# Attention scores of two softmax maps in three PSUM banks, and two banks in turn for transposed probabilities

## What the program must compute

```python
# group A: differential attention, per head; q and k split into two halves of 32
s1 = q[..., :32] @ k[..., :32].T * 32 ** -0.5
s2 = q[..., 32:] @ k[..., 32:].T * 32 ** -0.5
p  = softmax(s1) - lam * softmax(s2);      out_A = p @ v
# group D: attention over 512 latent keys with a window bias, and 256 context keys
p  = softmax(concat(q @ k_lat.T * 64 ** -0.5 + bias, q @ k_ctx.T * 64 ** -0.5));  out_D = p @ v
```

## Time and profile before

| | us |
|---|---|
| median of 3 executions | 5679.43 |
| lowest, highest | 5677.08, 5681.0 |
| the profiled execution | 5667.12 |
| its span, from first to last instruction | 5665.2 |
| `attend_stage` of layer 0, from the first product | about 450 to 676 |
| `attend_stage` of layer 1, from the first product | about 3633 to 3808 |

### The profile page before, as it was taken

The page is one execution under the profiler, slowest core; times in us unless marked ns, Lnnn a source line. Parts: engine busy times, 40 slices in busy tenths (PEclk is TensorE's granted clock), DMA queues, the critical chain, the costliest instruction groups (busy, mean ns, idle before and its releaser), DMA issues. The chain is left out here.

```text
span 5665.2 us, 93013 instructions
## 1 busy us (share of the span) xinstructions
PE 4687.9 (83%) x35878; PEld 2642.5 (47%) x35878; DVE 3514.7 (62%) x7609; ACT 1966.5 (35%) x5447; POOL 1761.5 (31%) x1767
## 2 busy tenths in 40 slices
PE   7988799768888797978877698779976978888777
PEld 3555599644334342524322255459964534334222
DVE  2776543468767677676764557554347776867644
ACT  1333333114343333434333223343321434343333
POOL 0210022004544444444443202003211454444432
PEclk8998899889999999999999999879988999999999
DMA  8756422429999999999999887312243999999998
GB/s 294 263 198 244 178 56 86 145 103 421 421 421 420 420 416 421 413 419 420 415 422 421 337 289 241 122 39 73 86 144 152 418 422 421 421 421 415 421 421 353
DMA packets 386541, 1729.76 MB, mean 305 GB/s; under 512 B 86216, under 2 KB 158456, under 8 KB 217976
## 3 DMA queue, kind: packets, MB, share of 16 engines
q0 software_dynamic: 195200, 1381.22, 59.3%
q1 hardware_dynamic: 163208, 281.69, 14.4%
q10 hardware_dynamic: 27696, 60.92, 3.0%
HBM read 1640.75 MB, written 86.65 MB: 305 GB/s over the span
## 5 line engine op out<-in xcount | busy, mean ns | idle before, releaser
L2419 PE MATMUL pe_ps<-pe_ring,pe_diag 128*128 128x512 f32 x5120 | 2455.0, 614 | 608.3 <-ACT pe_diag L2453 601.4
L2487 DVE SCALAR_TENSOR_TENSOR pe_ring<-pe_ring,ro_tb 128x1024 f32<-128x1024 f32 x1280 | 1561.5, 1225 | 935.0 <-DMA pe_ring<-in_peer_uv,ro_slot 913.5
L2066 POOL DMA_INDIRECT pe_ring<-in_peer_uv,ro_slot x1280 | 1443.3, 1128 | 2222.3 <-PE pe_ps L2419 1749.2
L2419 PEld LDWEIGHTS pe_ps<-pe_ring,pe_diag 128*128 128x128 f32 x5120 | 899.9, 191 | 2053.5 <-ACT pe_diag L2453 1326.9
L2447 ACT ACTIVATE pe_wts<-pe_raw 128x1 f32<-128x1 f32 x1280 | 258.4, 202 | 1744.9 <-DVE pe_ring L2487 1744.0
L929 PE MATMUL pp_ps<-pp_win,pp_uT 128*128 128x439 f32 (+6 forms) x1728 | 597.1, 504 | 8.0 <-issue 7.5
L2453 ACT ACTIVATE pe_diag<-c_ident,pe_wts 128x128 f32<-128x128 f32 x1280 | 513.9, 401 | 42.0
L929 PEld LDWEIGHTS pp_ps<-pp_win,pp_uT 128*128 128x128 f32 x1728 | 326.5, 195 | 263.9 <-issue 173.1
L2449 ACT ACTIVATE pe_wts<-pe_wts,ro_gates 128x1 f32<-128x1 f32 x1280 | 376.6, 294 | 41.6
L1372 POOL TENSOR_TENSOR ch_m<-ch_at,ch_joins 128x256 f32<-128x256 f32 x288 | 203.8, 744 | 472.6 <-DVE ch_at L1671 472.6
L2122 PEld LDWEIGHTS pe_ps<-ro_tbT,peer_wq 128*128 128x128 f32 x2048 | 248.8, 192 | 61.2 <-issue 61.2
(11 more groups left out here) (358 smaller groups left out, 5155.7 us busy)
## 6 DMA issues: line engine op xcount, KB each, us to landing
pp_win<-in_w_in SPq DMA_DIRECT2D x24, 1756.0 KB, 10.8
at_aw<-in_w_ada SPq DMA_DIRECT2D x10, 4096.0 KB, 13.3
pe_ring<-in_peer_uv,ro_slot POOLq DMA_INDIRECT x1280
ch_nat<-gd_dram SPq DMA_DIRECT2D x44, 448.0 KB, 4.1
gd_dram<-pp_gout POOLq DMA_DIRECT2D x40, 448.0 KB, 8.2
peer_wq<-in_peer_wq SPq DMA_DIRECT2D x8, 2048.0 KB, 8.5
rw_dram<-pp_out POOLq DMA_DIRECT2D x48, 320.0 KB, 5.2
ch_nat<-rw_dram SPq DMA_DIRECT2D x48, 320.0 KB, 4.1
```

The lines of the kernel that those rows point to most:

```text
L2066: return pool.indirect_dma_start(dst, None, table, bass.IndirectOffsetOnAxis(ap=index, axis=0))
L2419: mm = pe.matmul(ps[:, y_bank(p) + c, :], diag[:, n % DIAGS, :], ring[:, n % RING, D + c * 512:D + (c + 1) * 512], start=(k == 0), stop=(k ...
L2487: v.scalar_tensor_tensor(row, row, 1.0, tb[p % 2][:], ALU.mult, ALU.mult, accum_out=raw[p % 2][:, k:k + 1]).then_inc(dots_done, 1)
```

## The change

It has three edits. The two maps of group A are laid side by side in banks 0 to 2, 768 columns each, so that map 0 ends and map 1 begins in the middle of bank 1. `score_A` of a latent pair is issued in another order: map 0 keys 0 to 511 (bank 0), map 1 keys 256 to 767 (bank 2), map 0 keys 512 to 767 (the first half of bank 1); then PE waits for its own semaphore until that last product is done, and issues map 1 keys 0 to 255 (the second half of bank 1). Bank 3, which this leaves free, becomes a second bank for transposed probabilities: groups of transposes take banks 6 and 3 in turns, and each waits for the copy of the group before the last one only.

```diff
-        slotsA = ps[:, 0:4].rearrange("p (u a) b -> p u (a b)", u=2)
+        slotsA = ps[:, 0:3].rearrange("p a b -> p (a b)").rearrange("p (u k) -> p u k", u=2)
         slotD = ps[:, 4:6].rearrange("p a b -> p (a b)")
         ada_out = ps[:, 5, 256:512]
-        TURN, OUT = 6, 7
+        TURNS, OUT = (6, 3), 7
+        turn_bank = lambda job: TURNS[turn_at[job] % 2]
 ...
                 def score_A(x):
                     i, h = pairs[x]
                     if x:
                         pe.wait_ge(expA_done, 2 * x)
-                    for c0 in range(0, keys_of(x), 512):
-                        c1 = min(keys_of(x), c0 + 512)
-                        for u in range(2):
-                            at = 64 * (h % 2) + 32 * u
-                            mm = pe.matmul(slotsA[:, u, c0:c1], b["qA"][at:at + 32, h // 2, i * P:(i + 1) * P], b["kA"][at:at + 32, h // 2, c0:c1], start=True, stop=True)
-                            if c1 == keys_of(x):
-                                mm.then_inc(scoreA_done, 1)
+                    def map_scores(u, c0, c1):
+                        at = 64 * (h % 2) + 32 * u
+                        return pe.matmul(slotsA[:, u, c0:c1], b["qA"][at:at + 32, h // 2, i * P:(i + 1) * P], b["kA"][at:at + 32, h // 2, c0:c1], start=True, stop=True)
+                    if keys_of(x) == TOK:
+                        map_scores(0, 0, 512)
+                        map_scores(1, 256, TOK)
+                        map_scores(0, 512, TOK).then_inc(scoreA_done, 1)
+                        pe.wait_ge(scoreA_done, 2 * x + 1)
+                        map_scores(1, 0, 256).then_inc(scoreA_done, 1)
+                    else:
+                        map_scores(0, 0, CTX).then_inc(scoreA_done, 1)
+                        map_scores(1, 0, CTX).then_inc(scoreA_done, 1)
 ...
                 def turn(x, g, k):
                     n = turn_at[(x, g, k)]
                     pe.wait_ge((probsA_ready, probsD_ready)[g], x + 1)
-                    if n:
-                        pe.wait_ge(pt_ready, n)
+                    if n >= 2:
+                        pe.wait_ge(pt_ready, n - 1)
                     first, end = groups_of(x)[k]
                     for kt in range(first, end):
-                        tr = pe.transpose(ps[:, TURN, (kt - first) * P:(kt - first + 1) * P], ...
+                        tr = pe.transpose(ps[:, turn_bank((x, g, k)), (kt - first) * P:(kt - first + 1) * P], ...
```

More of the change, by code:

```diff
@@ L506, in turn @@
                     pe.wait_ge((probsA_ready, probsD_ready)[g], x + 1)
-                    if n:
-                        pe.wait_ge(pt_ready, n)
+                    if n >= 2:
+                        pe.wait_ge(pt_ready, n - 1)
                     first, end = groups_of(x)[k]
                     for kt in range(first, end):
-                        tr = pe.transpose(ps[:, TURN, (kt - first) * P:(kt - first + 1) * P], (pA, pD)[g][x % 2][:, kt * P:(kt + 1) * P], consts["ident"][:])
+                        tr = pe.transpose(ps[:, turn_bank((x, g, k)), (kt - first) * P:(kt - first + 1) * P], (pA, pD)[g][x % 2][:, kt * P:(kt + 1) * P], consts["ident"][:])
                     tr.then_inc(turned, 1)
@@ L591, in keep_turned @@
                         act.wait_ge(turned, turn_at[(x, g, k)] + 1)
-                        act.activation((ptA, ptD)[g][x % 2][:, first:end].rearrange("p k n -> p (k n)"), ps[:, TURN, 0:(end - first) * P], ACT.Copy).then_inc(pt_ready, 1)
+                        act.activation((ptA, ptD)[g][x % 2][:, first:end].rearrange("p k n -> p (k n)"), ps[:, turn_bank((x, g, k)), 0:(end - first) * P], ACT.Copy).then_inc(pt_ready, 1)
                 def root(m):
```

## The result

The changed kernel takes 5789.20 us (median of 5 executions, 5740.5 to 5799.07) against 5681.00 us before (5 executions, 5677.08 to 5682.89): the ratio is 1.0171, 95% interval 1.0141 to 1.0200. The profiled execution is the shortest of the five (5740.5; span 5738.3). Its span is 73 us above the 5665.2 of the profiled execution before, and these 73 us are what the trace can explain.

What follows compares the result with a forecast made beforehand. PE was taken to bound the attention stage; three-bank scores cost 27.7 us and the second transpose bank gains 20.1, so 7.6 us slower: 5679.4 + 7.6 = 5687 us, range 5666 to 5701.

Steps and rivals of the forecast that it cites:

- The full-clock arithmetic: Latent pairs of the attention stage: second bank gains 0.75 us a period, score_A costs 0.77 more; period 8.60 to 8.62.
- the second rival: In score_A the maps' 512-column pieces no longer run side by side: 32 us more, 5719 us; chance 0.05.
- 26 run at full clock and six at half: Clock split of the 32 latent scores, taken from the earlier trace; costs 20.0 and 7.7 us, 27.7 together.
- My own sign of being wrong: Period off by over 0.3 us, the 3.27 us gap no longer bringing half clock, or half clock seen elsewhere.
- the 3.27 us gap: PE idle before D0 of pair 12, layer 1; behind it the clock is at half for the stage's rest.
- The third rival: PE's own wait in score_A is expensive (1.05 us a score) or brings further half clock: 5696 to 5703; chance 0.15.
- the 0.77 us: Added full-clock cost of a latent score_A, 2.26 instead of 1.49 us, as map 1's last 256 columns run alone.

Runs made afterwards that it cites:

- the experiment with the squares: Kernel before, with the squares of the outputs on DVE moved from ahead of max_A to behind probs_A, root and norm one step later: 5664.74 us, ratio 0.9964.
- the partner: Changed kernel, with map 0's keys 0 to 255 computed a second time beside map 1's last piece, behind PE's wait: 5698.54 us, ratio 1.0039.
- the fast order: Changed kernel, with map 0 keys 512 to 767 and map 1 keys 256 to 767 issued before map 0 keys 0 to 511: 5645.95 us; again 5666.49.
- the filler: Changed kernel, with one needless 128x128 product on 256 columns before PE's wait for itself in each latent score: 5718.41 us, ratio 1.0068.

## Why the prediction was wrong

**The full-clock arithmetic held.** Weigh D starts 2.24 after score_A's start (2.26 forecast). The second bank was to bring score_A forward by 0.75 us a period, with a remaining wait of about 0.33 for ACT before weigh A. D0 follows A1 after 0.38 instead of the 0.44 I took, the wait is 0.25, and score_A comes 0.87 earlier: A1 to the next score_A is 3754.59 - 3751.65 = 2.94, against 534.96 - 531.15 = 3.81 in the earlier trace rows. The longer scores were to cost 0.77 and cost 2.24 - 1.49 = 0.75; at half clock they were to cost 1.29 and cost 4.13 - 2.86 = 1.27 (starts of score_A and of the product behind it). The period was forecast at 8.62 and is 8.48. The two maps still run side by side, so the second rival is out.

**The step that failed is the count "26 run at full clock and six at half".** It carried the clock of the old kernel over into the new one. With it the sum had each period's change right and left out that a period nearly doubles when the clock falls. The count is 17 and 15 in the profile after, and by their lower mean clock the longer executions have more. My own sign of being wrong, a half clock seen elsewhere than behind the 3.27 us gap, is what came.

**The third rival was the right one, and mis-sized.** It said that PE waiting for its drain and one map alone in the array could bring a further stretch at half clock, with 5696 to 5703 for the whole and a chance of 0.15. The price of such a stretch could have been worked out from the earlier trace rows: 15.5 - 8.6 = 6.9 us a pair. What I did not ask was how long a stretch lasts. At half clock PE is busy 99% of the time and the clock stays down; in layer 1 no ada_round follows before the stage ends, so one fall at pair 10 costs five periods, three more than before. The upper end of my range, 5701, had room for two.

**I looked for the fall at idle time only.** In the earlier trace rows it follows 3.27 us without work, and the experiment with the squares confirms that case. From there I took a shorter idle time to be safe. Idle time does matter: three of the five falls follow a wait of 1.08 us, and the three-bank scores lose the clock more often with one bank for transposes, which keeps ACT's waits (25 scores at half clock against 15). The Trainium skill (TensorE: Matmul & The Clock Gate, HAM oscillation — how this bites in real kernels) tells of the fall in the same way, as a matter of PE's pauses between bursts of work. This case's trace agrees for the 3.27 us and goes beyond that section for the rest: at 533 us the clock fell with PE busy in each of the windows shown, and the partner kept the clock longer by filling the array, with every wait left in place.

**The bank rule did not force the cost.** I weighed the rule that the prediction takes from the Trainium skill (TensorEngine Tiling (Array Packing), Restrictions and Gotchas), that two row tiles may not use one bank at the same time, as if it made the 0.77 us unavoidable. That skipped a choice that was mine, the order of the pieces. The rule was kept in the fast order as well, where the pieces meet the shared bank at different times, and the cost was nil. Whether two maps could use one bank at the same time was not tried.

What stays open: no run shows which quantity of the array's use decides the fall. That the lone map and the wait each bring more of it is shown, each by a run; that they do so by thinning the same stretch fits the filler and the order of all the medians, but is an inference. Nor is it shown why one execution of a program keeps the clock where another loses it.

## What to carry to other kernels

Before an edit that makes PE's work thinner (fewer partitions in use, a wait inside a group of products), price its clock as a term of its own: how many microseconds a period costs at the lower level, times the periods until work that is seen in the trace to bring the level back (here the ada_rounds). A busy PE was no protection here. And where two partition groups must share a bank, issue the pieces so that they come to it at different times before paying for a wait: the same four pieces cost 2.24 us in one order and 1.49 in another.

## What the runs showed of the hardware

- The two partition groups do not need equal pieces to run side by side: 256 columns of one beside 512 of the other, then the reverse, took 1.49 us for 768 columns each, the same as equal pairs.
- A wait of PE for its own product cost 0.34 us at full clock when the product before it was the one waited for, and nothing that shows when the two 512-column pieces lay between.
- The half-clock state lasted through periods of 15.25 us in which PE was busy 99%; each ada_round that began at half clock among the latent pairs ended at full clock. The changed kernel's time line of one such return, where the score_A before it (556.59) took 4.20 us:

```profile
564.11 5.12 PE L541 MATMUL at_ps<-at_aw,at_cond 128*32 128x256 f32 x64
...
573.58 2.30 PE L488 MATMUL at_ps<-at_kA,at_qA 32*128 32x512 f32 x8
```
